# Sample rows of the mLSTM laid by (head, token) over 128 partitions, routing by token tile, last weight load in halves

## The reference

```
s   = (q k^T) * exp(dmat - mt)                       # causal, inside one sequence
num = s @ v + exp(inter - mt) * (q @ c0)             # c0: stored 128x128 matrix, per sequence and head
den = sum(s) + exp(inter - mt) * (q @ n0)
h   = num / max(|den|, exp(-mt)); y = rmsnorm(h) * g * sigmoid(o)
c1  = decay * c0 + sum_s ws[s] * k[s] v[s]^T         # new matrix, returned
logits = x @ router_w + router_b; top_k(4); gates = softmax(top values)
out[token] = sum over its 4 experts of gate * (act(x @ w1 + b1) @ w2 + b2)
```

## Time and profile before

| | |
|---|---|
| median of 3 executions | 1213.25 us (1212.83 to 1213.63) |
| profiled execution: its own time | 1214.7 us |
| its span, first to last instruction | 1212.9 us |
| TensorE, VectorE, ScalarE, GpSimd busy | 94%, 30%, 14%, 12% of the span |
| read from HBM, written | 426.0 MB, 3.7 MB |
| mean granted TensorE clock | 0.969 of full |
| chain that ended last | PE 68%, DVE 13%, DMA 8%, SP's queue 7% |

### The profile page before, as it was taken

How to read it: one execution, slowest core, us unless ns; L and a number is a source line. 1 busy time by engine, 2 the same in 40 slices (tenths; PEclk the granted TensorE clock), 3 DMA queues, 4 the chain that set the end, 5 groups by cost and what they waited for, 6 DMA issues and landing times.

```text
span 1212.9 us, 13031 instructions
## 1 busy us (share of the span) xinstructions
PE 1144.4 (94%) x5046; PEld 480.0 (40%) x5046; DVE 365.3 (30%) x710; ACT 166.0 (14%) x315; POOL 140.5 (12%) x236
## 2 busy tenths in 40 slices
PE   7999877989999999999999999999999999999884
PEld 5767563453334333333433343333333332333221
DVE  5999873430212122131212121212121121202122
ACT  3312232111102010100110010102010100010002
POOL 6857853000000000000000000000000000000000
PEclk9999877978999999999999999999999999999998
DMA  7510643656999999999999999999999999999993
GB/s 223 198 46 1 208 162 134 216 224 250 427 427 426 427 427 427 427 428 428 428 428 428 428 428 428 428 428 428 428 428 428 428 428 428 428 428 427 427 427 122
DMA packets 78901, 430.13 MB, mean 355 GB/s; under 512 B 10714, under 2 KB 21186, under 8 KB 29714
## 3 DMA queue, kind: packets, MB, share of 16 engines
q1 hardware_dynamic: 78436, 428.47, 85.5%
q0 software_dynamic: 384, 1.18, 0.4%
q10 hardware_dynamic: 46, 0.01, 0.0%
HBM read 425.98 MB, written 3.67 MB: 354 GB/s over the span
## 4 chain that ended last, share of the span: by engine, by line
PE 68%; DVE 13%; DMA 8%; SPq 7%; issue 2%; ACT 1%; DVEq 0%; ACTq 0%
PE psum L1877 30%; PE psum L1887 14%; PE psum L1842 9%; SPq L360 6%; DMA ring_a<-in_exp_w_dram 5%; PE psum L1852 4%; DMA ring_b<-in_exp_w_dram 3%; PE psum L1739 2%; PE psum L1861 1%; PE psum L1898 1%; DVE ring_a L1140 1%; PE psum L1508 1%; DVE gsm L957 1%; PE psum L1730 1%; DVE ring_a L1136 1%
## 5 line engine op out<-in xcount | busy, mean ns | idle before, releaser
L1877 PE MATMUL psum<-ring_a,xg 128*64 128x512 f32 x1536 | 345.6, 599 | 7.8 <-DMA ring_a<-in_exp_w_dram 7.8
L1877 PEld LDWEIGHTS psum<-ring_a,xg 128*64 128x64 f32 x1536 | 105.5, 137 | 230.1 <-issue 213.2
L1887 PE MATMUL psum<-ring_a,aT 128*64 128x512 f32 x768 | 173.1, 597 | 8.3 <-DMA ring_a<-in_exp_w_dram 5.5
L1389 DVE TENSOR_TENSOR x<-x,psum 128x512 f32<-128x512 f32 x64 | 44.0, 687 | 365.7 <-PE psum L1852 365.7
L1842 PE MATMUL psum<-S,xn 128*128 128x256 f32 (+1 forms) x384 | 114.8, 429 | 1.2 <-DVE S L1377 1.2
L1877 PE MATMUL psum<-ring_b,xg 128*64 128x512 f32 x512 | 114.8, 595 | 0.2 <-DMA ring_b<-in_exp_w_dram 0.2
L1420 DVE TENSOR_SCALAR acts<-psum 128x512 f32<-128x512 f32 x32 | 22.0, 687 | 298.6 <-PE psum L1877 298.6
L1887 PEld LDWEIGHTS psum<-ring_a,aT 128*64 128x64 f32 x768 | 52.6, 136 | 110.0 <-issue 96.8
L1842 PEld LDWEIGHTS psum<-S,xn 128*128 128x128 f32 (+1 forms) x384 | 64.9, 195 | 57.3 <-issue 51.6
L1877 PEld LDWEIGHTS psum<-ring_b,xg 128*64 128x64 f32 x512 | 35.3, 137 | 73.6 <-issue 70.2
L865 ACT ACTIVATE acts<-acts 128x512 f32<-128x512 f32 x32 | 20.0, 626 | 316.6 <-DVE acts L1420 316.6
(11 more groups left out here) (414 smaller groups left out, 872.1 us busy)
## 6 DMA issues: line engine op xcount, KB each, us to landing
ring_a<-in_exp_w_dram SPq DMA_DIRECT2D x144, 2048.0 KB, 25.4
ring_b<-in_exp_w_dram SPq DMA_DIRECT2D x48, 2048.0 KB, 26.8
ring_a<-in_w_in_dram SPq DMA_DIRECT2D x5, 2048.0 KB, 8.6
...
```

What stands on the lines that cost most here:

```text
L1389: TT(dst, dst, psum[0:n, banks[c], :], ALU.add).then_inc(sem("combine_added"), 1)
L1877: m = M(psum[64 * x:64 * x + 64, bk, :], xg[:, k, u, 64 * x:64 * x + 64], w[:, 2048 * x + 512 * bk:2048 * x + 512 * bk + 512], start=False ...
L1887: m = M(psum[64 * x:64 * x + 64, 4 + nn, :], aT[:, 2 * j + s, 64 * x:64 * x + 64], w[:, 2048 * x + 1024 * s + 512 * nn:2048 * x + 1024 * s ...
```

## The change

1. **Sample rows by (head, token).** In all stages of the mLSTM the 32 sample rows of the four heads lie on partitions 32h to 32h+31: `v2` and `o2` (projected by `sample_tokens`, four column groups in turn), `k2`, the scores (`smp`), `E2`, the numerators and denominators (`nu2`, one bank, heads inside the loop over sequences), `vw`. Small operations of a head become one operation on 128 partitions. The factor of the old state is applied to q once (`qs`), and the result is spread with a mask (`bmask`) to `qm`; `scm` and its 8 copies go. GpSimd sets up the masks by more and smaller operations (some 20 more). The fills `rgT` and `s5T` move from the pool of six banks to banks 6 and 7, behind `ys0` and `ys1`.
2. **Memory updates in groups.** `memory_update(g)` issues the four heads of group g together, with 32 contracted partitions at 32h each: group 0 before the turn of y, groups 1 and 2 behind output matmuls 3 and 8. VectorE adds by group. The loads of `c0` are issued after use 4 of the `w_in` places (before: 5), step 1's after use 6.
3. **Routing by tile.** Tiles 0 and 2 have their logits in one bank and are routed while tile 1 is turned and multiplied (bank `lg1`); TensorE waits for its own last matmul of them (`logits_first`). The marks are made before the gates; the gates are made after `select`. The scaling of tile 1's rows moves behind the marks. Three fills with zero move ahead of the residual adds. `stay_busy` has 9 and 5 matmuls, with 128 contracted rows in place of 96.
4. **Count read early.** SyncE, ScalarE and VectorE read `most` before the sweep.
5. **Last step in halves.** The sweep's last load is two transfers of 1024 KB; TensorE's last step works on the first half while the second is under way. SyncE's last turn of the loop is written out.

The core of the diff (event lists, the masks of GpSimd, drains by ScalarE and the other call sites are left out):

```diff
+        rb = [ring_a[:], 6 * CH + 2 * H * NB - NB * 129]
+        vw = carve(rb, [128, NB, 129])
+        v2, E2 = v_tok[:, 2, 0, :], E[:, 0, 384:416]
...
+        k2 = k_tok[:, 2, 0:128]
...
+                if end:
+                    sp.dma_start(place[:, :, 0:1024], src[:, :, 0:1024]).then_inc(slot_filled(il)[0], 16)
+                    sp.dma_start(place[:, :, 1024:2048], src[:, :, 1024:2048]).then_inc(sem("end_filled"), 16)
+                else:
+                    sp.dma_start(place, src).then_inc(slot_filled(il)[0], 16)
...
-            sp.wait_ge(*at("w_in_used", 5))
+            sp.wait_ge(*at("w_in_used", 4))
...
+            sp.wait_ge(*at("w_in_used", 6))
             load_step(0, 1)
-            sp.wait_ge(*at("w_in_used", 6))
...
+            sp.wait_ge(*at("count_ready", 1))
+            most = sp.value_load(cnt[0:1, 0:1], min_val=0, max_val=T)
...
+            with sp.Fori(1, NPAIR // 2 - 1) as q:
+                load_pairs(q, q * (2 * STEPS))
+            load_pairs(NPAIR // 2 - 1, (NPAIR // 2 - 1) * (2 * STEPS))
...
+            po(g.memset(bmask[:], 1.0))
+            po(g.affine_select(out=bmask[:], in_=bmask[:], compare_op=ALU.is_ge, fill=0.0, base=0,
+                               pattern=[[-NT, NB], [1, TS]], channel_multiplier=0))
+            po(g.affine_select(out=bmask[:], in_=bmask[:], compare_op=ALU.is_ge, fill=0.0, base=NT - 1,
+                               pattern=[[NT, NB], [-1, TS]], channel_multiplier=0))
...
+            po(g.tensor_tensor(vw[:], spread(v2.unsqueeze(1), 1, NB), spread(wsm[:].unsqueeze(2), 2, 129), ALU.mult), "vw_ready")
...
+                    A(t_dve[:, 0:128], bank("nu2")[:, 0:128], ACT.Square, accum_out=rsm[:, 24:25]).then_inc(says_now("nsq_ready"), 1)
...
-            for b in range(NB):
-                V.tensor_copy(scm[:, b, NT * b:NT * b + NT], sd[:, NT * b:NT * b + NT]).then_inc(says_now("scm_ready"), 1)
...
-                drains(TSC(E[0:TS, h, 384:416], mb[0:TS, 256:288], rtok[0:TS, 2, h:h + 1], 0.0, ALU.subtract, ALU.max), f"mb{h}")
+                drains(TSC(E[:, h, 256:384], mb[:, 128:256], rtok[:, 1, h:h + 1], 0.0, ALU.subtract, ALU.max), f"mb{h}")
...
+            def e2_arg():
+                await_fill(dve, "smp")
+                says(TSC(E2, bank("smp")[:, 0:TS], rtok[:, 2, 0:1], 0.0, ALU.subtract, ALU.max), "e2_arg", 1)
+            def e2_prob():
+                dve.wait_ge(*at("e2_exp", 1))
+                dv(TT(E2, E2, causal[:, 384:416], ALU.mult))
+                drains(TT(E2, bank("smp")[:, TS:2 * TS], E2, ALU.mult), "smp")
...
-                drains(TT(qm[:, h], bank(f"sc{h}")[:, 0:NB * TS].rearrange("p (b t) -> p b t", b=NB),
-                          spread(qT[:, h, TP:T].unsqueeze(1), 1, NB), ALU.mult), f"sc{h}")
-            dve.sem_inc(says_now("qm_ready"), 1)
+            await_fill(dve, "sc")
+            qs = t_dve[:, 0:H * TS].rearrange("p (h t) -> p h t", h=H)
+            drains(TT(qs, bank("sc")[:, 0:H * TS].rearrange("p (h t) -> p h t", h=H), qT[:, :, TP:T], ALU.mult), "sc")
+            says(TT(qm[:], spread(qs.unsqueeze(2), 2, NB), spread(bmask[:].unsqueeze(1), 1, H), ALU.mult), "qm_ready", 1)
...
+            def sample_denominators():
+                await_fill(dve, "nu2")
+                den, out = bank("nu2")[:, 128:129], rsm[:, 56:57]
+                dv(V.tensor_copy(out, den))
+                dv(STT(out=out, in0=den, scalar=-1.0, in1=out, op0=ALU.mult, op1=ALU.max))
+                says(TT(out, out, rtok[:, 2, 1:2], ALU.max), "den_read", 3)
...
+                if part == 2:
+                    drains(STT(out=o2, in0=bank("nu2")[:, 0:128], scalar=rv, in1=o2, op0=ALU.mult, op1=ALU.mult), "nu2")
+                    dve.sem_inc(says_now("y3_ready"), 1)
...
+            dv(V.memset(lg[:], 0.0))
+            dv(V.memset(slot[:], 0.0))
+            dv(V.memset(sgate[:], 0.0))
...
+            dve.wait_ge(sem("logits_first"), 1)
+            for i in (0, 2):
+                ins_ = logits(i, bank("lg")[0:TILES[i][1], NE * i:NE * i + NE])
+                drains(ins_, "lg") if i == 2 else dv(ins_)
+            for i in (0, 2):
+                best(i)
+            dv(choose(slice(0, 3, 2), 2))
+            dve.wait_ge(*at("root2_ready", 3))
+            dv(V.reciprocal(st2[:, 5:6], st2[:, 5:6]))
+            await_fill(dve, "lg1")
+            drains(logits(1, bank("lg1")[:, 0:NE]), "lg1")
+            best(1)
+            says(choose(slice(1, 2), 1), "mask_ready", 1)
             says(TT(gk[:, :, 0:TOPK], top[:, :, 0:TOPK], spread(top[:, :, 0:1], 2, TOPK), ALU.subtract), "top_diff", 1)
-            chosen, weighted = (v.rearrange("p i x s -> p i (x s)").rearrange("p i (k e) -> p i k e", k=TOPK) for v in (S[:, 0], SG[:]))
-            by_choice = lambda v: spread(v[:, :, 0:TOPK].unsqueeze(3), 3, NE)
-            dv(TT(chosen, spread(spread(iota_e[:].unsqueeze(1).unsqueeze(1), 1, 3), 2, TOPK), by_choice(topf), ALU.is_equal))
-            dv(V.tensor_reduce(msk[:], chosen.rearrange("p i k e -> p i e k"), AX.X, ALU.add))
-            says(V.tensor_copy(mskb[:], msk[:]), "mask_ready", 1)
-            dve.wait_ge(*at("top_exp", 1))
-            dv(V.tensor_reduce(gk[:, :, 4:5], gk[:, :, 0:TOPK], AX.X, ALU.add))
-            dv(V.reciprocal(gk[:, :, 4:5], gk[:, :, 4:5]))
-            dv(TT(gk[:, :, 0:TOPK], gk[:, :, 0:TOPK], spread(gk[:, :, 4:5], 2, TOPK), ALU.mult))
-            dv(TT(weighted, chosen, by_choice(gk), ALU.mult))
-            dv(V.tensor_reduce(gts[:], weighted.rearrange("p i k e -> p i e k"), AX.X, ALU.add))
+            for hf in range(2):
+                await_fill(dve, f"h2T{2 + hf}")
+            dv(TSC(xn[:, 1, :], xn[:, 1, :], st2[:, 5:6], None, ALU.mult))
...
             select(0).then_inc(sem("s_ready"), 1)
+            select_bias(0).then_inc(sem("selb_ready"), 1)
             dv(V.tensor_reduce(st2[:, 8:9], bank("cum")[:, 96:128], AX.X, ALU.max))
             says(V.tensor_copy(cnt[:], st2[:, 8:9]), "count_ready", 1)
-            select_bias(0).then_inc(sem("selb_ready"), 1)
+            dve.wait_ge(*at("top_exp", 1))
+            dv(V.tensor_reduce(gk[:, :, 4:5], gk[:, :, 0:TOPK], AX.X, ALU.add))
+            dv(V.reciprocal(gk[:, :, 4:5], gk[:, :, 4:5]))
+            dv(TT(gk[:, :, 0:TOPK], gk[:, :, 0:TOPK], spread(gk[:, :, 4:5], 2, TOPK), ALU.mult))
+            dv(TT(weighted, chosen, by_choice(gk, slice(0, 3)), ALU.mult))
+            dv(V.tensor_reduce(gts[:], weighted.rearrange("p i k e -> p i e k"), AX.X, ALU.add))
+            for i0, i1, n in parts:
+                dv(V.tensor_copy(pairs(sgate, i0, i1, n), src(gts[0:n, i0:i1, :])))
             dve.wait_ge(sem("s_ready"), 1)
+            most = dve.value_load(cnt[0:1, 0:1], min_val=0, max_val=T)
             sweep(0)
-            most = dve.value_load(cnt[0:1, 0:1], min_val=0, max_val=T)
...
+            def sample_tokens(name, halves):
+                await_bank(pe, name)
+                for k in range(KD):
+                    for h in range(H):
+                        c, col = halves[h // 2]
+                        w = slot_view(c % 3, WCH[c][1])
+                        m = M(bank(name)[TS * h:TS * h + TS, 0:128], hT[:, k, TP:T], w[:, k, col + 128 * (h % 2):col + 128 * (h % 2) + 128],
+                              start=(k == 0), stop=(k == KD - 1))
...
+            def sample_scores():
+                await_bank(pe, "smp")
+                M(bank("smp")[:, 0:TS], selh[:].rearrange("k h t -> k (h t)"), gsm[0:H, 4, TP:T], start=True, stop=True)
+                for h in range(H):
+                    m = M(bank("smp")[TS * h:TS * h + TS, TS:2 * TS], kT[:, h, TP:T], qT[:, h, TP:T], start=True, stop=True)
+                ends_fill(m, "smp")
...
+                if i == 2:
+                    await_bank(pe, "nu2")
+                    for h in range(H):
+                        r = slice(TS * h, TS * h + TS)
+                        M(bank("nu2")[r, 0:129], E2[r, :], v2[r, :], start=True, stop=False)
+                    for b in range(NB):
+                        for h in range(H):
+                            m = M(bank("nu2")[TS * h:TS * h + TS, 0:129], qm[:, h, b, :], c0[:, h, b, :], start=False, stop=(b == NB - 1))
+                    ends_fill(m, "nu2")
...
+            def memory_update(g):
                 b0, b1 = CB[g]
-                pe.wait_ge(*at("vw_ready", h + 1))
-                name = f"cu{h}{g}"
-                await_bank(pe, name)
-                ends_fill(M(bank(name)[:, 0:(b1 - b0) * 129], k_tok[0:TS, 2, 128 * h:128 * h + 128],
-                            vw[:, h, b0:b1, :].rearrange("p b v -> p (b v)"), start=True, stop=True), name)
+                pe.wait_ge(*at("vw_ready", 1))
+                for h in range(H):
+                    name, r = f"cu{h}{g}", slice(TS * h, TS * h + TS)
+                    await_bank(pe, name)
+                    ends_fill(M(bank(name)[:, 0:(b1 - b0) * 129], k2[r, :], vw[r, b0:b1, :].rearrange("p b v -> p (b v)"),
```

(22 more changed lines are left out.)

328 lines of the change are left out of this document (157 added, 171 removed), and 6 rows, old and new, of the table b.

## The result

The changed kernel takes 1184.41 us (median of 4 runs, 1184.34 to 1186.5) against 1213.04 us before (4 runs, 1212.3 to 1213.63): ratio 0.9765, interval 0.9753 to 0.9777, 28.6 us less. The profiled execution took 1186.5 us (span 1184.8), so between the two profiles lie 28.2 us where the prediction had 32.9.

The account below looks back on a forecast made before the run. The weight stream at 424 GB/s bounds the kernel, so gains before its first waiting load count in full. Terms summed to 32.9 us: 1214.7 to 1181.8, less 1.45 for the median, rounded 1180 us; range 1173 to 1192.

Parts of the forecast that it names:

- The bound and the shape: Whole kernel: the 909.6 us weight stream stays unchanged; time won before the first waiting load is won in full.
- Setup and `scm`: Start of the kernel: GpSimd's added mask work costs 0; removing eight VectorE copies to `scm` gains 0.7 us.
- Scores, `qm`, GELU argument, numerators of tile 1: Up to the gated outputs of tiles 0 and 1: 5.5 us gained; lead (time by which points come earlier) 6.2.
- The factors of tile 2: VectorE's tiny operations: decays start about 9.3 us earlier, four operations again wait for one each; lead 9.3, bounds 6 and 12.
- the numerators' own speed: Sample numerators of tile 2 on TensorE: about 2 us in place of 7.8, of which 2.1 us counted as gain.
- Outputs and updates of tile 0: TensorE's outputs of tile 0 with memory updates: 19.8 us in place of 28.6, gain 8.8, bounds 5.4 and 9.8.
- The stores "move along": VectorE's residual add waits for the small states' stores; that chain was to move along with updates and outputs, 0 change.
- are absorbed by one wait that I take to move along, the stores of the small states: Rival at the small states' stores: they stay at 233 us, only routing and tail gain 5.8 us, 1207 us; chance 0.03.
- Routing: From the last logits to the first gather: routing by tile and gates behind `select` gain 3.3 us, bounds 2.3 and 4.
- The clock: First gather to first waiting load: shorter TensorE idle times around the counts keep full clock, gain 9.0 us.
- That it might fall: Rival around the counts: the clock falls all the same, price 9.0 us, giving 1189 us; chance 0.28.
- End: Tail after the last landing: halved last step gains 1.8 us, VectorE's count read leaving gains 0.7 us.

Follow-up runs that it names:

- e10: Changed kernel with GpSimd's decays held back until VectorE's y3_ready and the four new-memory stores issued behind the router's loads and small stores: 1173.26 us.
- e3: Changed kernel with GpSimd's four decays of c0 held back until VectorE has said rg_used: 1179.03 us.
- e1: Changed kernel with GpSimd's four decays of c0 held back until VectorE has said s5_gelu: 1180.83 us.
- e2: Changed kernel with GpSimd's four decays of c0 held back until VectorE has said y3_ready: 1177.12 us.
- e4: Changed kernel with the 32 sample numerator products ordered head by head instead of the four heads in turn: 1184.48 us.
- run 11: Changed kernel with decays held until y3_ready, new-memory stores behind the router's loads, and six small identity matmuls ahead of the projections: 1174.72 us.
- e5: Changed kernel without the 9 and 5 filling matmuls around the counts: 1191.76 us.
- run 6: Changed kernel with the eight memory updates of groups 1 and 2 issued one by one between outputs of tile 0: 1185.78 us.
- Run 7: Changed kernel with the four stores of the new memory issued behind the router's loads and the two small stores: 1180.52 us.
- run 8: Changed kernel with the last load in one piece, its step in the old order, and VectorE's count read behind its sweep again: 1185.63 us.
- e9: Changed kernel with filling matmuls reading 96 rows of the rounded bias, numbers 9 and 5 kept: six executions, 1182.1 to 1192.4 us.
- e12: Changed kernel with filling matmuls reading 96 rows of ones instead of 128, numbers 9 and 5 kept: five executions, 1182.24 to 1191.3 us.

## Why the prediction was right, and where its steps were not

*The bound and the shape.* Right: all that was won lies ahead of the first waiting load and in the tail, and the stream took 910.0 us for 909.6.

*Setup and `scm`.* The 0.7 us cannot be seen: `mix_ready` came 1.9 us later. This is no cost of the change. It depends on the execution. In some, TensorE's projections start at 687 ns each and fall to 406 ns at a moment that differs. That is the clock. Beware of the view here: it gives a granted clock of 1.00 for the slow matmuls too, but the trace's own list of clock stretches only begins at the moment in the table, at full clock, and for the time ahead of it nothing was recorded. Where the list begins early enough it shows them: in e10 it begins at 12.3 us, the matmuls ran at 406 ns, then at up to 687 ns from 15.7 to 19.1 us, and a window there (columns as in the earlier trace rows) gives 0.50:

```profile
15.80:19.00 3.20, 3.20 (x8) 2.20 (x8) 0.78 (x5) 2.10 (x6) 2.70 (x9) 0.50 0.39 106
```

| kernel | clock list begins, at full clock | `mix_ready` |
|---|---|---|
| before | 17.0 us | 142.37 |
| after | 20.5 us | 144.29 |
| e3 | 20.0 us | 143.96 |
| e1 | 17.2 us | 142.18 |
| e2, e4 | 12.7, 13.4 us | 141.32, 140.96 |

Executions with the same moment (before and e1) differ by 0.2 us. The other three executions after the change have spans of 1182.6 to 1182.7 us, 2.1 us under the profiled one, as such a difference would make it. The Trainium skill ("TensorE: Matmul & The Clock Gate", Part 1) says that the number of matmuls at the lower speed changes from run to run of one kernel; these rows agree. What sets the moment here stays open; run 11 shows that filling the idle time before the projections does not bring it forward.

*Scores, `qm`, GELU argument, numerators of tile 1.* Right, 5.9 us for 5.5 up to the gated outputs. `qm` took 2.54 us beside `vw`, of which 1.1 was to be waiting.

*The factors of tile 2: the step that failed.* As it put it, the decays "start about 9.3 us earlier, and four VectorE operations again wait for one each". The decays did start 9.3 us earlier against `mix_ready`. But what stood beside them was no longer the tiny operations; it was the product of 128x576 ahead of them, which ended only at 183.3 us, 0.6 us after the third of the four decays, and took TensorE's `glu`, and so ScalarE's sigmoids, along. The lead grew by 0.7 us here, not 3.1. Runs 1 to 3 show cause and price. The 2.1 us that I had counted for the numerators' own speed are not to be seen: VectorE reads them 12.4 us after their end, and even in run 4, at three times their length, 2.8 us after.
By the Trainium skill ("SBUF — State Buffer", Who interferes with whom) whoever issues first holds the shared ports for its whole operation; by that rule the product should have waited for one operation of GpSimd's, the one then running, and not for several. Most rows agree: the tiny operations of run 1 and the last product of run 2 waited only until the decay then running had ended, though the next was queued behind it. The product of the changed kernel does not: it waited 6.4 us, through the rest of the bias subtraction and three decays. It did so in all seven traces in which the first decay starts straight behind the bias subtraction (after, e5 to e9, e12: 7.12 to 7.14 us), and in none of the seven others (1.52 to 1.54 us); in e4 the pause between the two was 0.08 us. Why it loses its turn three times, no run shows.

*Outputs and updates of tile 0: mis-sized the other way.* Sum 19.8 us, measured 15.7; gain 12.7 for 8.8. I had left 3 us for half clock, and in the profiled execution the clock was full from the first output; I had 2.5 us for eight updates, and they took 1.65. The first is in part luck of the execution: in the traces of runs 1, 4, 7 and 8 the first four outputs ran at a granted clock of 0.55 to 0.70, and the stretch took 17.3 to 18.6 us.

*The stores "move along".* Wrong by 1.7 us. Of these 0.6 us are the three zero fills, which I had taken to run beside TensorE's work and which stood ahead of the first residual add; the other 1.1 us are the longer wait for the stores. The rival that the leads "are absorbed by one wait that I take to move along, the stores of the small states" named the right place with a mechanism that was not it: they don't stay at 233 us, they come later behind other stores. Run 7 shows it, and run 6 that grouping the eight updates was worth only 1.5 us because of it.

*Routing.* The routing itself gave what was forecast: from the end of tile 1's outputs to the gather it took 14.2 us before and 11.1 after, 3.1 for 3.3. The stretch gave 1.4 because tile 1's second half ran 1.7 us longer, 8.83 us, at a granted clock of 0.81 where it was 1.00 before: a loss of clock that my sum had put at nothing. In runs 1, 6, 7, 8, 10 and 11 it took 7.13 us, in runs 2, 3, 4, 5, 9 and 12 8.6 to 8.8. The longer ones follow TensorE's stop of 1.4 to 1.6 us at the turns, but runs 1 and 8 have the stop and 7.13 us; without the stop (runs 6, 7, 10, 11) it was always 7.13. What decides between the two stays open.

*The clock.* Right for the gather, 8.9 us for 9.0, and run 5 gives its price a second time. That it might fall was given 0.28; runs 9 and 12, with other operands in the filling, show that this was no idle doubt, though with the changed kernel's own filling it held in 49 of 50 executions.

*End.* 2.1 for 2.5.
